# Gate matrices of the PEER stage: column order inside the PSUM bank

## The reference

```python
q = (h @ wq).reshape(B, S, H, PEER_QDIM)
s1 = einsum('bshd,hnd->bshn', q[..., :half], k1); s2 = the same with the other half and k2
v1, i1 = top_k(s1, 16); v2, i2 = top_k(s2, 16)          # 16 first keys, 16 second keys
cand = v1[..., :, None] + v2[..., None, :]; top_s, pos = top_k(cand, 16)
gates = softmax(top_s)                                  # 8 heads x 16 experts for a token
act = gelu(einsum('td,tkd->tk', xc, u[ec]))             # only the chosen experts
y = einsum('tk,tkd->td', act * gc, v[ec])
```

## Time and profile before

| what | value |
|---|---|
| time, median of 3 runs | 2177.69 us (2177.17 to 2179.45) |
| time of the profiled execution | 2180.03 us |
| its span in the trace | 2178.1 us |
| granted TensorE clock, mean over the span | 0.991 of full speed |
| PE busy | 2102.3 us, 97% |
| DVE busy | 1664.2 us, 76% |
| ACT busy | 1239.9 us, 57% |
| POOL busy | 243.1 us, 11% |

### The profile page before, as it was taken

The page is one execution under the profiler, slowest core; times in us unless marked ns, Lnnn a source line. Parts: engine busy times, 40 slices in busy tenths (PEclk is TensorE's granted clock), DMA queues, the critical chain, the costliest instruction groups (busy, mean ns, idle before and its releaser), DMA issues.

```text
span 2178.1 us, 41640 instructions
## 1 busy us (share of the span) xinstructions
PE 2102.3 (97%) x14556; PEld 1945.3 (89%) x14556; DVE 1664.2 (76%) x3071; ACT 1239.9 (57%) x2289; POOL 243.1 (11%) x196
## 2 busy tenths in 40 slices
PE   3999899999999999999989999999999999999998
PEld 2899899999999988888879998999999998888886
DVE  7786869998788788888765765899978886666665
ACT  2467455545777644444455664555477775444444
POOL 0000000000665300000000000000045560000000
PEclk7999999999999999999999999999999999999999
DMA  7764645555444488888654445555544435655553
GB/s 309 261 215 140 213 155 176 183 183 174 136 136 132 160 288 288 291 289 290 231 183 160 157 135 166 165 184 182 184 156 128 134 129 174 193 194 192 193 193 121
DMA packets 114185, 412.48 MB, mean 189 GB/s; under 512 B 13264, under 2 KB 13904, under 8 KB 113424
## 3 DMA queue, kind: packets, MB, share of 16 engines
q1 hardware_dynamic: 114064, 410.86, 56.4%
HBM read 406.48 MB, written 1.57 MB: 187 GB/s over the span
## 4 chain that ended last, share of the span: by engine, by line
PE 91%; DVE 4%; ACT 3%; DMA 1%; issue 1%; SPq 0%; DVEq 0%; ACTq 0%
PE ps L1449 32%; PE ps L1145 15%; PE ps L1149 15%; PE ps L1146 15%; PE ps L1428 5%; PE ps L1214 2%; ACT w_hi L439 1%; PE ps L1197 1%; PE ps L1369 1%; DVE w_lo L699 1%; DMA raw<-in_win 1%; PE ps L1402 1%; PE ps L1303 1%; DVE big L774 1%; DVE big L753 1%
## 5 line engine op out<-in xcount | busy, mean ns | idle before, releaser
L699 DVE TENSOR_TENSOR w_lo<-raw,w_hi 128x1024 fp32r<-128x1024 f32 x664 | 811.0, 1222 | 282.6 <-ACT w_hi L439 280.6
L439 ACT CAST w_hi<-raw 128x1024 fp32r<-128x1024 f32 x664 | 695.0, 1047 | 514.7 <-PE ps L1149 441.4
L1145 PE MATMUL ps<-h_hi,w_hi 128*128 128x256 f32 x2912 | 723.6, 286 | 1.7 <-ACT big L444 1.5
L1146 PE MATMUL ps<-h_lo,w_hi 128*128 128x256 f32 x2912 | 713.6, 283 | 0.0
L1145 PEld LDWEIGHTS ps<-h_hi,w_hi 128*128 128x128 f32 x2912 | 560.2, 192 | 5.6 <-issue 2.6
L1146 PEld LDWEIGHTS ps<-h_lo,w_hi 128*128 128x128 f32 x2912 | 558.2, 192 | 0.1
L425 POOL TENSOR_SCALAR hot<-con,rt 128x128 f32<-128x128 f32 x192 | 243.0, 1276 | 1553.3 <-DVE neg L1089 1414.8
L1149 PE MATMUL ps<-h_hi,w_lo 128*128 128x256 f32 x2912 | 408.8, 283 | 4.3 <-DVE w_lo L699 4.3
L1149 PEld LDWEIGHTS ps<-h_hi,w_lo 128*128 128x128 f32 x2912 | 375.6, 192 | 5.0 <-DVE w_lo L699 4.9
L630 ACT CAST p_hi<-big 128x256 fp32r (+1 forms) x256 | 103.8, 406 | 343.2 <-PE ps L1449 343.2
L1449 PE MATMUL ps<-w_hi,p_hi 128*128 128x512 f32 x1024 | 274.9, 389 | 0.2
(11 more groups left out here) (188 smaller groups left out, 1704.9 us busy)
## 6 DMA issues: line engine op xcount, KB each, us to landing
raw<-in_u SPq DMA_DIRECT2D x256, 512.0 KB, 3.5
raw<-in_v SPq DMA_DIRECT2D x256, 512.0 KB, 4.1
raw<-in_win SPq DMA_DIRECT2D x104, 512.0 KB, 3.9
hot<-in_ada SPq DMA_DIRECT2D x80, 512.0 KB, 4.2
raw<-in_wq SPq DMA_DIRECT2D x32, 512.0 KB, 3.5
big<-in_ada SPq DMA_DIRECT2D x16, 512.0 KB, 14.5
raw<-in_wout SPq DMA_DIRECT2D x16, 512.0 KB, 4.2
big<-in_decay SPq DMA_DIRECT2D x2, 1536.0 KB, 12.0
```

What stands on the lines that cost most here:

```text
L439: nc.scalar.copy(w_hi[:, j % 2, :], raw[:, j, :]).then_inc(hi_ready, 1)
L699: tt(w_lo[:, j % 2, :], raw[:, j, :], w_hi[:, j % 2, :].bitcast(F32), ALU.subtract).then_inc(lo_ready, 1)
L1145: mm(o, w, h_hi[:, k, :], start=(k == 0), stop=False)
L1146: mm(o, w, h_lo[:, k, :], start=False, stop=False)
```

## The change

Two access patterns change, and no instruction is added or removed. Before, the four tokens of a bank are interleaved: column i of token t lies at element 4 i + t, so a matmul's 128 output columns lie 16 bytes apart, and four tokens' values of one i are neighbours. Afterwards token t owns the elements 128 t to 128 t + 127 of the bank, so a matmul writes a contiguous run. The multiplication still runs over i, then the two banks, then the four tokens, as `acts` demands. Its reads from the bank now go 128 elements (512 bytes) from one token to the next instead of one element.

```diff
-                    g8 = ps[:, 2 + 2 * (b % 2):4 + 2 * (b % 2), :].rearrange("p h (i t) -> p i h t", t=BATCH // 2)
+                    g8 = ps[:, 2 + 2 * (b % 2):4 + 2 * (b % 2), :].rearrange("p h (t i) -> p i h t", t=BATCH // 2)
                     tt(a8, a8, g8, ALU.mult).then_inc(gate_used, 1)
...
-                            o = bank(2 + 2 * (b % 2) + h).rearrange("p (i t) -> p t i", t=BATCH // 2)[:, t, :]
+                            o = bank(2 + 2 * (b % 2) + h)[:, P * t:P * (t + 1)]
                             k = BATCH // 2 * h + t
```

## The result

The changed kernel takes 2127.63 us (median of 4 runs, 2127.0 to 2131.08), the kernel before, in runs beside it, 2178.57. The ratio is 0.9768 with a 95% interval of 0.9756 to 0.9781: 51 us, or 2.3%, faster. 41 us had been forecast, and the time lies 1.6 us above the low end of the stated range.

The account below looks back on a forecast made before the run. PE was taken to bound the kernel. Gate matmuls were to save 41.3 us, with nothing counted for the faster PE's effects or the multiplication: 2136.4 us against the 2177.69 median, range 2126 to 2186.

Parts of the forecast that it names:

- The bound: Gate batches in both layers: PE without idle stretch for some 202 us, so time off PE is time off the kernel.
- The matmul: Gate matmuls (L1428): the strided write costs 53 ns extra of 107; contiguous they start every 66 ns, saving 41.3 us.
- the ceiling: Gate matmul spacing at most 80 ns, from a batch's first start interval; a batch then costs 1.32 us, saving 28 us.
- The size: Saving over 64 gate batches: each 1.11 us in place of 1.755, 41.3 us in all.
- the floor that the prediction gave: Gate matmul spacing at least 56 ns, its columns plus 2 to 3 ns; a batch costs 0.96 us, saving 51 us.
- its signs: Expected profile: sixteen L1428 matmuls in 1.1 to 1.3 us, not 1.92; stage about 181 us, not 202; L1051 at 1221 ns.
- What the faster PE meets: Stage with batches: DVE, ACT and POOL still fit a 10.86 us cycle of three blocks; nothing counted against the saving.
- The 5 us kept for ACT's late steps: Upper bound for `w_hi` coming up to 1.5 us late behind ACT's one-hot rows; counted as nothing in the sum.
- The multiplication: VectorE's `weigh` (L1051), jumping 512 bytes per element on its bank operand: zero extra taken, 1.6 us the far end.
- The slower rival: L1051 costs over 1.22 us more each, VectorE becomes the bound and the kernel slower; 2203 us at +1.6 us; chance 0.14.
- the prediction's last part: Sign for L1051: at over 1.8 us DVE is busy for the whole stage and PE waits for `w_lo`.

Follow-up runs that it names:

- the run with the blocks inside: Against the changed kernel, VectorE's multiplication walks banks and tokens outside, the 128 blocks inside: bank read contiguously, `acts` in SBUF jumping 1 KB; 2191.22 us, ratio 1.0051.
- with 1.13 us added: Against the changed kernel, an unused VectorE sum over 1024 elements added ahead of the one-hot rows of each batch; 2172.8 us, ratio 0.9964.
- the runs with pairs: Against the changed kernel, each token's columns written in runs of two neighbours, 32 bytes from run to run; 2126.38 us, ratio 0.9756.

## Why the prediction was right

- **The bound.** PE was the bound before and is after. The reading of one stage instead of the means held.
- **The matmul.** That the strided output, not the weight load, doubled it was argued from two start intervals of a batch. It is now shown: the write alone brings the gain, and matmuls of half the columns cost 55 ns, about half of 107. One detail of the argument was read wrongly. The first interval of 80 ns was taken as the ceiling of what a matmul with its load might cost. After the change it is 70 ns ahead of a steady 56, so it said nothing of the steady rate. And two rows were misread without harm: the 122 ns of L1402 are busy time by count, while sixteen of them in 1.95 us start (1.95 - 0.275) / 15 = 112 ns apart, and L1197's mean of 434 ns holds the slow ones of the first 25 us, up to 765 ns (its median is 379). That such a plain float32 matmul streams at about half speed stands.
- **The size, which was off.** The term was 66 ns for a start, taken from the projections' 13 ns over their columns. Measured are 56, the floor that the prediction gave. So the sixteen in 1.07 us and the stage of 177 us came out just below its signs (1.1 to 1.3 us, 181 us). A batch costs (10.54 - 8.64) / 2 = 0.95 us in place of the predicted 1.11 and the 1.755 before, and 64 x 0.805 = 51.5 us. That is the 51.8 us of the spans. The trace had a warning. The matmuls of 512 columns in the output stage are over their columns by as much; here they are after the change:

```profile
850.90 1.07 PE L1449 MATMUL ps<-w_hi,p_lo 128*128 128x512 f32 x4
```

  (1.07 - 0.39) / 3 = 227 ns for 213 ns of columns: 14 over, with twice the columns to hide a load. So the 13 ns look like a fixed price of each of these float32r matmuls and not like one of load and stream as such, and the gate's float16 matmul showed 2 to 3 ns of its own already before. What makes the 13 ns stays open. The 81 ns that the Trainium skill (TensorE: Matmul & The Clock Gate, "Back-to-back issue gap") gives for 128 columns with a load each were not met: 56 ns, its bare gap, with a load ahead of every one.
- **What the faster PE meets.** Nothing, as forecast. PE has no gap between 549.5 and 727 us. The 5 us kept for ACT's late steps were not needed.
- **The multiplication.** Taken at zero, measured at zero. The reason given (the bank serves a lone element every 0.83 ns on PE's side, and VectorE asks for one every 1.05) fits all runs, but no run tests it as a cause. The warning on SBUF by the Trainium skill (Vector Engine (DVE) Microarchitecture Reference, "Measured stream behaviour on trn2") doesn't carry over to PSUM. On SBUF it holds (in the run with the blocks inside, where the output jumps too), and at 2.4 ns nearer its highest row (2.50) than the 1.73 that the prediction used.
- **The slower rival.** Its threshold was 0.58 us for VectorE to become the bound and 1.22 for a loss. Measured are 0.3 in a full cycle, since PE's cycle came out shorter and VectorE needs 9.9 us and not 9.7, and about 1.2: with 1.13 us added the ratio is 0.9964, with 1.37 us more for each multiplication it is 1.0051. But PE would not have waited for `w_lo`, as the prediction's last part had it. In both runs it waited for the one-hot rows. They are the last item in VectorE's step and `w_lo` is the first, while PE wants `w_lo` only 585.92 - 584.96 = 0.96 us before them.

## What to carry to other kernels

When a matmul's spacing is twice its columns, look at where its output lands before looking at its operands. Here an output in aligned pairs of float32 was all that full speed needed, and VectorE, which reads the bank, could take the jump for nothing. Which side of a layout may jump depends on the memory: on PSUM the VectorE read was free, and in SBUF a jump at every element, in an operand and in the output, cost more than the whole change had gained. And when an overhead is borrowed from another instruction, check it on a second size of that instruction first, since that tells an overhead of the pair from one of the data type.

## What the runs showed of the hardware

- A float16 matmul wrote to PSUM at 0.83 ns for an element alone in its aligned 8 bytes and at full rate (56 ns for 128 columns) as soon as two neighbours shared them. Steps of 8 and of 16 bytes and pairs at odd elements all gave 107 ns. The Trainium skill (PSUM — Partial Sum Buffer, "Specifications (TRN2)") names 8-byte lines, which fits. The same row says that any pattern that isn't contiguous slows matmuls, which the runs with pairs contradict: 32 bytes between runs cost nothing.
- A VectorE multiplication of 1024 elements took 1222 ns with runs of four, runs of two and no neighbours at all in its PSUM operand, and 2594 ns with a jump of 1 KB at every element in its SBUF operand and output. A VectorE sum of 1215 ns held up the next instruction for 1.13 us.
- The gate's weight loads went from a mean of 134 to 98 ns with nothing changed about them, and the shortest took 96 and 95. The duration of a load in the profile contains its wait for the matmul ahead.
